# The first tile's gate, output rows and norm set apart from the second tile's in a two-layer decoder trunk

## Chip, cores and metric

One NeuronCore of a Trainium2 chip (trn2) runs the whole program. The metric is the device time of one execution in microseconds (us), here the median of three.

## What is computed

Two layers over 512 tokens of width 1024, float32, causal. Each layer is a token mixer with a residual and an expert FFN (PEER) with a residual, each behind an RMSNorm. Layer 0 mixes with HGRN2 (four heads of 128) and an S5 state-space model (32 groups, 64 states) whose output is gated; layer 1 with a gated DeltaNet. Cut to the parts around the change:

```python
# layer 0: the S5 half ends in a gate, then one output projection over both halves
y = gelu(y)
y = y * sigmoid(y @ glu_w)                      # "u" half of the mixer's output
h = h + concat(hgrn_out, y) @ ev_out_w          # output rows
# PEER FFN of both layers
xn = rmsnorm(h, norm_ffn_w)
q = (xn @ w_q).reshape(n_tok, 8, 2, 128)        # 8 heads, two halves
scores = einsum('thcd,ckd->thck', q, sub_keys)
top_s, top_i = top_k(scores, 16)                # then top 16 of the 256 sums
act = gelu(einsum('td,tkd->tk', xn, u_tab[expert_id]))
h = h + einsum('tk,tkd->td', gate * act, v_tab[expert_id])
```

## The kernel before, in words

Tokens lie along the free axis, channels on the 128 partitions. The mixer works on two groups of 256 tokens (g = 0, 1), the FFN on four tiles of 128 tokens. One round is one head of one tile: 16 slots, and in each slot GpSimd gathers 128 rows of 8 KB (the u and v rows of one expert for each token) into a ring of 8 (later 15) slots in SBUF (`gather`, L674 to 688), VectorE forms the dot products with the tile's rows (`dot`, L2318), ScalarE makes gelu and gate of two slots (`gelus`, L1523) and TensorE adds the weighted v rows in PSUM (`values`, L796), which releases the ring slots (`v_free`). There are 64 rounds, 1024 gathers. The ring's first eight slots (`ring`, L467) lie over the memory of the layer-0 mixer: slots 0 and 1 over chunks 0 to 3 of the output weights `first_w` (L384), slot 2 over `glu_w2[0]`, slots 3 to 5 over the S5 buffers, slots 6 and 7 over chunks 4 to 7 of `first_w`. So GpSimd waits before its first gather for `first_mm` = 4, which says that the output rows of both tiles of group 0 are done.

The order of work on each engine is written out by hand. `Paced` objects (L297) hold the steps of one piece of work with due slots, counted in slots of the round loop; negative slots, run through in a loop up to 0, are the stage ahead of the first gather. At each half slot the parts are called in the order of their list. `spread` (L140) maps the raw slots of the second group's mixer to slots, `query_at` (L87) sets where a query projection stands, `side_order` (L269) lists who uses the PSUM bank `side` and when. SyncE loads the weights through a ring of four (L594), each when the fourth before it has been used.

Ahead of the first gather, group 0 goes through the mixer. The norm of group 1 is made meanwhile (`second_norm`: squares on ScalarE from slot -112, L1440; eight matmuls with the mean matrix on TensorE at -104, L709; root on ScalarE, L1448), and applied on VectorE behind the gate (`mixer_in(1)`, L1944). `first_glu` (PE L1102, ACT L1655) makes the product with `glu_w` and the sigmoid for the whole group, `glu(0)` (L2197) the gate. Then TensorE runs `first_rows` (L1029) for tile 0 and tile 1 of the group interleaved: 4 k-blocks of a tile and one chunk of outputs are 4 matmuls; a float32 matmul shows as two records. VectorE adds the residual (`first_added`, L2215), ScalarE squares, TensorE sums (`first_sum`, L1046), ScalarE makes the root, VectorE applies it (`first_apply`, L1944), TensorE makes head 0's query (`first_query`, L1058) and scores (L1066). VectorE then routes (`route(0)`, L2239 to 2310), TensorE spreads the ids over the tile's blocks (`across`, L791), VectorE writes them (L2315), and the first gather goes. Behind it TensorE broadcasts the tile's rows (`first_tile_rows`, 32-row matmuls of 512 columns, L770; ScalarE copies them, L1508), sums tile 1's squares, and runs the queries of heads 0 and 1 for tile 1 (`two_heads`, L1080). These lines set the order on TensorE between the loops:

```python
first_rows(1, low, range(3))
pe.wait_ge(s["mixu_ready"], 2)
first_rows(0, high, range(DC))
first_rows(1, low, range(3, 6))
first_sum(0)
first_rows(1, low, range(6, DC))
first_rows(1, high, range(2))
first_query(0)
```

## Time and profile before

| | us |
|---|---|
| median of 3 runs | 3036.7 |
| lowest, highest | 3035.95, 3038.07 |
| span of the profiled execution | 3036.9 |
| TensorE, VectorE, ScalarE, GpSimd busy | 2117.2, 2207.9, 1402.1, 1164.2 |
| gathers: share of the 16 DMA engines' span | 85.8% |

The span runs from the first to the last instruction of the profiled execution; the page gives no other time of it, and it lies between the lowest and the highest of the three runs. No engine is busy for more than 73% of the span, while the DMA engines are busy most of it; the page's slices say where. Times in the rows below are in us from the span's start. PE is TensorE, PEld its weight loads, DVE VectorE, ACT ScalarE, POOL GpSimd, SP SyncE; PEclk is TensorE's granted clock as a share of 2.4 GHz.

### The profile page before, as it was taken

The page shows a single profiled execution, that of the slowest core. Times are in us where ns is not written, and L with a number is a line of the kernel's source. Part 1 is how long each engine was busy: PE and PEld are TensorE (multiplying, and loading weights), DVE is VectorE, ACT ScalarE, POOL GpSimd, SP SyncE. Part 2 cuts the span into 40 slices and gives each one's busy share as a digit, 9 for nine tenths or more (in the row PEclk, how much of TensorE's full clock was granted, in tenths as well). Part 3 has the DMA queues.
Part 4 walks back from the last instruction along what each step waited for, and adds up shares of the span by engine and source line. Part 5 has one row for each costly group of instructions (what it writes and reads, how often), then busy time and mean ns, then how long its engine had stood idle before and what let it go on. Part 6 is the DMA issues. An engine that isn't in the chain of part 4 may idle for free.

```text
span 3036.9 us, 39024 instructions
## 1 busy us (share of the span) xinstructions
PE 2117.2 (70%) x13544; PEld 1275.4 (42%) x13544; DVE 2207.9 (73%) x6050; ACT 1402.1 (46%) x3425; POOL 1164.2 (38%) x1041
## 2 busy tenths in 40 slices
PE   7989877674667688687776888868775655453334
PEld 6876544350334456455543655545442311120001
DVE  8767888767666878777666678878866766667774
ACT  3434455433234766674333476667433422342222
POOL 0013344444344434434334344344445344443342
PEclk8989887885789899988887889999886866575555
DMA  6239999999999999999999999999999999999997
GB/s 221 70 135 417 419 419 420 412 419 419 418 417 394 420 397 412 420 366 405 418 419 419 398 401 418 420 405 390 421 417 420 420 421 421 421 421 422 421 421 299
DMA packets 182422, 1185.28 MB, mean 390 GB/s; under 512 B 19664, under 2 KB 25808, under 8 KB 50896
## 3 DMA queue, kind: packets, MB, share of 16 engines
q0 software_dynamic: 147456, 1073.81, 85.8%
q1 hardware_dynamic: 34768, 108.98, 9.3%
q8 instruction: 107, 1.75, 0.2%
q14 instruction: 91, 0.75, 0.1%
HBM read 1180.61 MB, written 2.10 MB: 389 GB/s over the span
## 4 chain that ended last, share of the span: by engine, by line
DMA 43%; PE 28%; DVE 10%; ACT 9%; issue 5%; POOL 5%; another core or an unknown queue 0%; SPq 0%; DVEq 0%; ACTq 0%; POOLq 0%
DMA arena<-uv_tab,cols 42%; PE ps L805 7%; PE xps L728 6%; POOL arena L685 5%; DVE arena L2327 4%; PE ps L728 4%; ACT L1532 2%; ACT scr L1532 2%; PE xps L1214 2%; ACT scr L1536 1%; PE xps L1265 1%; PE ps L780 1%; DVE arena L2424 1%; PE xps L1288 1%; PE xps L1285 1%
## 5 line engine op out<-in xcount | busy, mean ns | idle before, releaser
L685 POOL DMA_INDIRECT arena<-uv_tab,cols x1024 | 1160.0, 1133 | 1828.0 <-PE ps L805 1265.0
L2327 DVE CUSTOM_DVE_ANT_0 arena<-arena 128x1024 f32<-128x1024 f32 x1024 | 1251.5, 1223 | 660.8 <-DMA arena<-uv_tab,cols 633.2
L805 PE MATMUL ps<-arena,scr 128*32 128x512 f32 x4096 | 717.6, 782 | 679.0 <-ACT scr L1536 649.1
L1532 ACT ACTIVATE scr<-sel,cols 128x32 f32<-128x32 f32 x1024 | 272.9, 314 | 1111.0 <-DVE cols L2327 1081.3
L805 PEld LDWEIGHTS ps<-arena,scr 128*32 128x32 f32 x4096 | 92.2, 121 | 1002.0 <-ACT scr L1536 897.2
L728 PE MATMUL xps<-arena,wring 128*128 128x256 f32 x1600 | 401.2, 401 | 8.7 <-DVE arena L2485 4.2
L728 PEld LDWEIGHTS xps<-arena,wring 128*128 128x128 f32 x1600 | 308.8, 200 | 102.9 <-issue 46.4
L728 PE MATMUL ps<-arena,wring 128*128 128x256 f32 x1152 | 293.6, 414 | 14.2 <-ACT arena L1497 7.6
L1536 ACT ACTIVATE scr<-scr,cols 128x32 f32<-128x32 f32 x1024 | 273.0, 313 | 16.6
L728 PEld LDWEIGHTS ps<-arena,wring 128*128 128x128 f32 x1152 | 235.1, 209 | 97.6 <-issue 41.9
L1532 ACT ACT_TABLE_LOAD x154 | 197.6, 1283 | 2.7
L780 PE MATMUL ps<-ident,arena 128*32 128x128 f32 x1792 | 75.7, 322 | 31.7 <-ACT arena L1515 25.9
L780 PEld LDWEIGHTS ps<-ident,arena 128*32 128x32 f32 x1792 | 60.9, 132 | 85.0 <-ACT arena L1515 56.3
L1265 PE MATMUL xps<-arena 128*128 128x128 f32 x448 | 69.1, 301 | 25.7 <-DVE arena L2437 23.1
L1265 PEld LDWEIGHTS xps<-arena 128*128 128x128 f32 x448 | 59.4, 205 | 62.0 <-DVE arena L2437 39.0
L2327 DVE DVE_READ_ACCUMULATOR2_ANT cols<- 128x1 f32 x1024 | 84.2, 82 | 0.0
L1521 ACT ACT_TABLE_LOAD x61 | 78.3, 1283 | 1.1
L2244 DVE FIND_INDEX8 cols<-cols,arena 128x8 uint32<-128x128 f32 x256 | 69.8, 285 | 0.0
L1515 ACT ACTIVATE arena<-ps 128x512 f32<-128x512 f32 x56 | 33.2, 594 | 78.1 <-PE ps L780 47.9
L2424 DVE SCALAR_TENSOR_TENSOR arena<-arena,consts 128x256 f32<-128x256 f32 x144 | 63.2, 480 | 7.2 <-ACT arena L1748 6.6
L1214 PE MATMUL xps<-arena 128*128 128x256 f32 x256 | 63.0, 397 | 6.7 <-DMA arena<-wall 6.7
L2239 DVE MAX8 cols<-arena 128x8 f32<-128x128 f32 x256 | 61.7, 283 | 7.5 <-ACT arena L1689 5.8
(462 smaller groups left out, 2713.3 us busy)
## 6 DMA issues: line engine op xcount, KB each, us to landing
wring<-wall SPq DMA_DIRECT2D x176, 512.0 KB
arena<-uv_tab,cols POOLq DMA_INDIRECT x1024
arena<-wall SPq DMA_DIRECT2D x16, 512.0 KB, 7.9
h<-xT SPq DMA_DIRECT2D x2, 1024.0 KB, 10.6
arena<-glu_w SPq DMA_DIRECT2D x2, 1024.0 KB
out<-arena SPq DMA_DIRECT2D x3, 512.0 KB
arena<-s_b SPq DMA_DIRECT2D x1, 512.0 KB, 9.0
arena<-s_bt SPq DMA_DIRECT2D x1, 512.0 KB, 9.7
```

Source lines behind the costliest of these rows:

```text
L685: pool.indirect_dma_start(out=whole_row(at), out_offset=None, in_=uv_tab, in_offset=bass.IndirectOffsetOnAxis(ap=ids[g % 2][:, k:k + 1], a ...
L728: mm = pe.matmul(o, wring[:, n % NSLOT, k, :], rhs[k], start=(first and k == 0), stop=(k == DC - 1), skip_group_check=True)
L780: mm = pe.matmul(side[32 * e:32 * e + 32, tl(k)], xn[:, 4 * (i % 2) + k, at:at + 32], ident[:, :], start=True, stop=True, skip_group_check ...
L805: mm = pe.matmul(ps[4 + half][32 * c:32 * c + 32, :], wdiag[:, b % PAIRS, j, :], pair_row(at + j, 1)[:, T * half:T * half + T], start=(g % ...
L1214: mm = pe.matmul(o, z_w[c][:, k, :], hm[:, k, :], start=(k == 0), stop=(k == DC - 1), skip_group_check=True)
L1265: mm = pe.matmul(ps[2][:, tl(j)], negA[:, tl(j)], inv[:, tl(j)], start=(j == 0), stop=(j == 3), skip_group_check=True)
L1521: act.activation(soft_e, sel_v, ACT.Exp, bias=soft_m, accum_out=soft_s).then_inc(s["soft_exp"], 1)
L1532: m = act.activation(wdiag[:, b % PAIRS, n % 2, :], place, ACT.Gelu, scale=dots[g % 2][:, n:n + 1])
L1536: m = act.activation(wdiag[:, b % PAIRS, n % 2, :], wdiag[:, b % PAIRS, n % 2, :], ACT.Copy, scale=gate[g % 2][:, n:n + 1])
L2244: m = dve.max_index(top_i[:, c, lo:lo + 8], top_v[:, c, lo:lo + 8], keyed[:, c, :])
L2327: dve.tensor_tensor_reduce(u, u, xrep[:, block_of(k), :], 1.0, 0.0, ALU.mult, ALU.add, dots[g % 2][:, k:k + 1]).then_inc(s["dot_done"], 1)
L2424: mm = stt(o, raw_in(i)[:, e, j:j + GT], conv_w[:, GH * i + 2 * p + e, j:j + 1], o, ALU.mult, ALU.add)
```

## The change

- Group 1's norm: its squares on ScalarE move from slot -112 to -83, into another buffer (`halves1`), its eight matmuls on TensorE from -104 to both sides of `first_sum(0)`, its root behind that of the first tile, its application on VectorE from behind the gate to behind the scaling of tile 0.
- `first_glu` is made by tile and not by output block; the sigmoids and the gate of tile 0 come first, each of half the size.
- The rows of tile 1 are no longer made ahead of tile 0's: 16 of their 64 matmuls stand behind tile 0's first query, 48 among the eight `first_tile_rows`. The residual add, the norm and the two heads' queries of tile 1 move to slots 3 to 9 of round 0.
- Tile 0's norm is applied in two steps, the product with the weight ahead of the root.
- Gathers use the ring turned by two slots, so that the first two take slots 2 and 3; gather 0 waits for `first_mm` = 2, gather 4 for 3, gather 6 for 4.
- Group 1's mixer starts at slot 11 and not 8 with a spread of 1.04 and not 1.05, head 2's query of group 0 at 12 and not 8, and `route(2)` runs in slots 18 to 21, three steps a slot, and no longer from slot 14.

The diff, cut to its core:

```diff
@@ -89,7 +89,7 @@
-    return 16 * r + (8 if r == 0 else 9 if r % 8 == 0 and r > 0 else 2)
+    return 16 * r + (12 if r == 0 else 9 if r % 8 == 0 and r > 0 else 2)
@@ -149,7 +149,7 @@
-SPREAD = {"even": (1, 8, 1.05, math.inf, 0), 0: (264, 264, 1.02, 380, 8), 1: (524, 524, 1.03, 637, 8)}
+SPREAD = {"even": (1, 11, 1.04, math.inf, 0), 0: (264, 264, 1.02, 380, 8), 1: (524, 524, 1.03, 637, 8)}
@@ -194,7 +194,7 @@
 def slot_of(at):
-    return at % NS if at < LONG_FROM else (at - LONG_FROM) % NS_LONG
+    return (at + 2) % NS if at < LONG_FROM else (at - LONG_FROM + 2) % NS_LONG
@@ -268,7 +268,7 @@
 def side_order():
-    todo = [(-10, "q", 0, -1), (-9, "sc", 0, -1), (-8, "q", 0, -2), (-7, "sc", 0, -2), (4.5, "q", 0, 0), (6.7, "sc", 0, 0)]
+    todo = [(-10, "q", 0, -1), (-9, "sc", 0, -1), (-8, "q", 0, -2), (-7, "sc", 0, -2), (8.5, "q", 0, 0), (10.7, "sc", 0, 0)]
@@ -380,7 +380,7 @@
-        halves1 = region(0, DC, GT)
+        halves1 = region(26112, DC, GT)
@@ -677,7 +677,9 @@
-            pool.wait_ge(s["first_mm"], 4)
+            pool.wait_ge(s["first_mm"], 2)
+    if g == 0 and k in (4, 6):
+        pool.wait_ge(s["first_mm"], 1 + k // 2)
@@ -701,23 +703,18 @@
         def _(pe):
-def norm_sum(g):
-    for k in range(DC):
+def norm_sum(g, ks):
+    for k in ks:
...
-        mm = pe.matmul(ps[(2, 6)[g]][:, 0:GT], mean_d[:, :], (halves, halves1)[g][:, k, :], start=(k == 0),
+        mm = pe.matmul(ps[(2, 0)[g]][:, 0:GT], mean_d[:, :], (halves, halves1)[g][:, k, :], start=(k == 0),
...
-    mm.then_inc(s["sum_ready"], 1)
+    if k == DC - 1:
+        mm.then_inc(s["sum_ready"], 1)
...
-norm_sum(0)
-def second_norm():
-    pe.wait_ge(s["u_ready"], 4)
-    norm_sum(1)
-    yield 0
+norm_sum(0, range(DC))
@@ -756,7 +753,8 @@
 def first_tokens():
-    pe.wait_ge(s["xn_first"], 1)
+    pe.wait_ge(s["xn_first"], 2)
+    pe.wait_ge(s["root_ready"], 2)
@@ -797,6 +795,8 @@
+    if g == 0 and b == 0:
+        pe.wait_ge(s["out_added"], 4)
@@ -1040,21 +1040,23 @@
 def first_sum(t):
-    for k in range(DC):
-        if k % 4 == 0:
-            pe.wait_ge(s["hsq_ready"], 2 * t + k // 4 + 1)
-        mm = pe.matmul(ps[(3, 5)[t]][:, 0:P], mean_d[:, :], first_sq2[t][:, k, :], start=(k == 0),
-                       stop=(k == DC - 1))
+    for n in range(DC):
+        k = n if t == 0 else (n + 4) % DC
+        if n % 4 == 0:
+            pe.wait_ge(s["hsq_ready"], 2 * t + n // 4 + 1)
+        mm = pe.matmul(ps[3][:, 0:P], mean_d[:, :], first_sq2[t][:, k, :], start=(n == 0),
+                       stop=(n == DC - 1))
...
 def first_query(hd):
...
-    pe.wait_ge(s["xn_first"], 1)
...
+            if k % 4 == 0 and c == 0:
+                pe.wait_ge(s["xn_first"], k // 4 + 1)
@@ -1066,6 +1068,11 @@
+def tile_one_sum():
+    first_sum(1)
+    yield 0
@@ -1101,32 +1108,27 @@
 def first_glu():
-    def part(ks, n):
-        o = ps[(0, 5)[n // 2]][:, GT * (n % 2):GT * (n % 2) + GT]
+    def part(ks, t):
...
-            mm = pe.matmul(o, glu_w2[0][:, k, P * n:P * n + P], uT[:, k, :], start=(n % 2 + k == 0),
-                           stop=(k == 3), skip_group_check=True)
+            for n in range(4):
+                mm = pe.matmul(ps[(0, 5)[t]][:, tl(n)], glu_w2[0][:, k, P * n:P * n + P], uT[:, k, tl(t)],
+                               start=(n + k == 0), stop=(k == 3), skip_group_check=True)
...
-    pe.wait_ge(s["root_ready"], 2)
-    for n in (0, 1):
-        part(range(3), n)
+    part(range(3), 0)
...
-    for n in (2, 3):
-        part(range(3), n)
+    part(range(3), 1)
...
-    for n in range(4):
-        mm = part((3,), n)
-        if n % 2:
-            mm.then_inc(s["s5_glu"], 1)
+    for t in range(2):
+        part((3,), t).then_inc(s["s5_glu"], 1)
@@ -1348,7 +1350,7 @@
-        pe.wait_ge(s["mixu_ready"], 3)
+        pe.wait_ge(s["mixu_ready"], 5)
@@ -1366,11 +1368,11 @@
-paced += [Paced(-147.5, pair_weights()), Paced(-104, second_norm())]
+paced += [Paced(-147.5, pair_weights())]
...
-paced += [Paced(-80, first_glu()), Paced(mixed_at(1) + 1, glu(1), g_slot(1)), Paced(3.25, two_heads())]
+paced += [Paced(-80, first_glu()), Paced(mixed_at(1) + 1, glu(1), g_slot(1)), Paced(4.5, tile_one_sum()), Paced(7.25, two_heads())]
@@ -1381,24 +1383,29 @@
-pe.wait_ge(s["s5_xy"], ST)
-first_rows(1, low, range(3))
...
-first_rows(1, low, range(3, 6))
+pe.wait_ge(s["s5_sig"], 2)
+norm_sum(1, low)
...
-first_rows(1, low, range(6, DC))
-first_rows(1, high, range(2))
+norm_sum(1, high)
...
-first_rows(1, high, range(2, DC))
+pe.wait_ge(s["s5_xy"], ST)
+first_rows(1, low, high)
...
+pe.wait_ge(s["mixu_ready"], 4)
...
-first_sum(1)
+    if i < 4:
+        first_rows(1, high, (4 + i,))
+    elif i < 6:
+        first_rows(1, low, range(2 * i - 8, 2 * i - 6))
+    else:
+        first_rows(1, high, range(2 * i - 12, 2 * i - 10))
@@ -1444,16 +1451,14 @@
-    root = (trt, nrt)[g]
-    own.link(act.activation(root, ps[(2, 6)[g]][:, 0:GT], ACT.Ln, bias=eps_col))
-    act.activation(root, root, ACT.Exp, scale=-0.5).then_inc(s["root_ready"], 1)
-def second_norm():
-    act.wait_ge(s["mixh_ready"], 1)
+    own.link(act.activation(trt, ps[(2, 0)[g]][:, 0:GT], ACT.Ln, bias=eps_col))
+    act.activation(trt, trt, ACT.Exp, scale=-0.5).then_inc(s["root_ready"], 1)
+def second_squares():
+    act.wait_ge(s["e_mm"], 20)
...
-    yield 12
-    norm_root(1)
+    yield 0
@@ -1659,22 +1664,24 @@
-    for i in range(2):
-        yield 14 + i
-        act.wait_ge(s["s5_glu"], i + 1)
-        act.activation(sg[:, 2 * i:2 * i + 2, :], heads2(ps[(0, 5)[i]][:, :]),
-                       ACT.Sigmoid).then_inc(s["s5_sig"], 1)
+    for t in range(2):
+        for i in range(2):
+            yield 14 + 2 * t + i
+            act.wait_ge(s["s5_glu"], t + 1)
+            act.activation(sg[:, 2 * i:2 * i + 2, tl(t)], tiles4(ps[(0, 5)[t]][:, :])[:, 2 * i:2 * i + 2, :],
+                           ACT.Sigmoid).then_inc(s["s5_sig"], 1)
 def first_norm(t):
-    for i in range(2):
-        act.wait_ge(s["out_added"], 2 * t + i + 1)
+    for n in range(2):
+        i = (n, 1 - n)[t]
+        act.wait_ge(s["out_added"], 2 * t + n + 1)
...
+    yield 1.5
...
-    act.wait_ge(s["hm_ready"], 4)
-    own.link(act.activation(nrt[:, tl(t)], ps[(3, 5)[t]][:, 0:P], ACT.Ln, bias=eps_col))
+    own.link(act.activation(nrt[:, tl(t)], ps[3][:, 0:P], ACT.Ln, bias=eps_col))
@@ -1859,10 +1866,10 @@
-paced += [Paced(-147, pair_weights()), Paced(-112, second_norm())]
+paced += [Paced(-147, pair_weights()), Paced(-83, second_squares())]
...
-paced += [Paced(-81.5, first_glu()), Paced(mixed_at(1), glu(1), g_slot(1)), Paced(5.25, two_heads())]
+paced += [Paced(-81.5, first_glu()), Paced(mixed_at(1), glu(1), g_slot(1)), Paced(4, first_norm(1)), Paced(9.25, two_heads())]
@@ -1871,7 +1878,9 @@
-first_norm(0)
+for _ in first_norm(0):
+    pass
+norm_root(1)
@@ -1881,7 +1890,6 @@
-first_norm(1)
@@ -1991,7 +1999,7 @@
-        norm_apply(0, (trt, nrt)[g], h[:, :, own_tokens(g)], hm,
+        norm_apply(0, trt, h[:, :, own_tokens(g)], hm,
@@ -2197,29 +2205,51 @@
 def glu(g):
+    if g:
+        dve.wait_ge(s["s5_sig"], 6)
+        for i in range(2):
+            x = uT[:, 2 * i:2 * i + 2, :]
+            mm = tt(x, x, sg[:, 2 * i:2 * i + 2, :], ALU.mult)
+        mm.then_inc(s["mixu_ready"], 1)
+    else:
+        first_gate(0)
+def first_gate(t):
...
-        dve.wait_ge(s["s5_sig"], 2 * g + (2 if g else i + 1))
-        x = uT[:, 2 * i:2 * i + 2, :]
-        mm = tt(x, x, sg[:, 2 * i:2 * i + 2, :], ALU.mult)
-        if i or g == 0:
-            mm.then_inc(s["mixu_ready"], 1)
-    if g == 0:
-        mixer_in(1)
+        dve.wait_ge(s["s5_sig"], 2 * t + i + 1)
+        x = uT[:, 2 * i:2 * i + 2, tl(t)]
+        tt(x, x, sg[:, 2 * i:2 * i + 2, tl(t)], ALU.mult).then_inc(s["mixu_ready"], 1)
 def first_added(t):
...
-    for i in range(2):
-        dve.wait_ge(s["first_mm"], 2 * t + i + 1)
+    for n in range(2):
+        i = (n, 1 - n)[t]
+        dve.wait_ge(s["first_mm"], 2 * t + n + 1)
...
+def first_weighted(i):
+    dve.wait_ge(s["out_added"], i + 1)
+    mark(tt(xn[:, 4 * i:4 * i + 4, tl(0)], h[:, 4 * i:4 * i + 4, tl(0)],
+            norm_w[:, 1, 4 * i:4 * i + 4].unsqueeze(2).to_broadcast([P, 4, P]), ALU.mult))
+def first_scaled():
+    settled()
+    dve.wait_ge(s["h_root"], 1)
+    for i in range(2):
+        x = xn[:, 4 * i:4 * i + 4, tl(0)]
+        tt(x, x, nrt[:, tl(0)].unsqueeze(1).to_broadcast([P, 4, P]), ALU.mult).then_inc(s["xn_first"], 1)
 def first_apply(t):
...
-               range(DC)).then_inc(s[("xn_first", "xn_ready")[t]], 1)
+               range(DC)).then_inc(s["xn_ready"], 1)
@@ -2535,12 +2565,15 @@
+first_gate(1)
...
-first_apply(0)
+for i in range(2):
+    first_weighted(i)
+first_scaled()
+mixer_in(1)
...
-first_added(1)
@@ -2548,17 +2581,23 @@
-        if r == 0 and k == 1:
+        if r == 0 and k == 3:
+            first_added(1)
+        if r == 0 and k == 5:
...
-        if k == (14 if r % PH == 0 else ROUTE_SLOT):
+        if r and k == (14 if r % PH == 0 else ROUTE_SLOT):
...
+        if r == 1 and k == 2:
+            nxt = route(2)
...
-        if k % 2 == 0:
+        if k % 2 == 0 or r == 1 and k < 5:
+            next(nxt, None)
+        if r == 1 and k < 5:
```

## Rows read from the trace of the kernel before

**Rows 1.** The page, section 2: slices of 75.9 us (1/40 of the span).
```profile
PEclk8989887885789899988887889999886866575555
DMA  6239999999999999999999999999999999999997
GB/s 221 70 135 417 419 419 420 412 419 419 418 417 394 420 397 412 420 366 405 418 419 419 398 401 418 420 405 390 421 417 420 420 421 421 421 421 422 421 421 299
```
**Rows 2.** The page, section 3: queue, packets, MB, share.
```profile
q0 software_dynamic: 147456, 1073.81, 85.8%
```
**Rows 3.** Windows: length, busy us of each engine (instructions), PEclk, DMA share, GB/s.
```profile
118.00:124.00 6.00, 5.72 (x62) 4.16 (x61) 1.88 (x6) 4.43 (x6) 0.00 (x0) 1.00 0.28 90
...
200.00:203.00 3.00, 3.00 (x10) 1.23 (x9) 2.90 (x14) 1.56 (x3) 2.38 (x3) 0.97 0.46 93
203.00:210.00 7.00, 7.00 (x11) 2.60 (x10) 4.71 (x16) 3.00 (x6) 5.47 (x6) 0.50 0.98 404
...
200.00:220.00 20.00, 15.59 (x44) 7.48 (x43) 10.95 (x39) 11.43 (x20) 8.68 (x8) 0.66 0.92 367
220.00:235.00 15.00, 14.51 (x109) 11.91 (x106) 12.86 (x36) 7.16 (x22) 6.08 (x6) 0.89 1.00 385
250.00:600.00 350.00, 273.43 (x1782) 170.81 (x1775) 290.37 (x865) 176.10 (x407) 144.29 (x124) 0.85 1.01 418
```
**Rows 4.** Timeline, GpSimd: start us, us, line, what, idle before and its releaser.
```profile
200.01 1.09 POOL L685 DMA_INDIRECT arena<-uv_tab,cols  x1 [195.43 <-DVE cols L2315]
...
220.63 0.93 POOL L685 DMA_INDIRECT arena<-uv_tab,cols  x1 [9.81 <-PE ps L805]
...
285.25 0.94 POOL L685 DMA_INDIRECT arena<-uv_tab,cols  x1 [10.53 <-PE ps L805]
```
**Rows 5.** Chain that ended last, 0 to 260 us: start us, us, what.
```profile
112.19 3.65 PE ps L709 x16
...
165.94 2.68 PE xps L1036 x24
168.62 3.57 PE ps L1036 x32
172.19 4.47 PE xps L1036 x40
...
180.23 1.79 PE ps L1036 x16
...
183.81 3.59 PE ps L1058 x32
...
200.47 10.46 PE xps L770 x16
```
**Rows 6.** Timeline: ScalarE, VectorE and TensorE, 100 to 166 us.
```profile
101.87 2.00 ACT L1440 ACTIVATE arena<-h 128x1024 f32<-128x1024 f32 x2
...
148.25 0.38 ACT L1647 ACTIVATE arena<-ps 128x256 f32<-128x256 f32 x1 [10.07 <-PE ps L1022]
...
150.71 0.42 ACT L1653 ACTIVATE arena<-arena 128x256 f32<-128x256 f32 x1
...
151.34 0.48 DVE L2193 SCALAR_TENSOR_TENSOR arena<-ps,consts,arena 128x256 f32<-128x256 f32 x1
...
161.31 0.50 PE L945 MATMUL xps<-arena 128*128 128x128 f32 x2 [0.74 <-DVE arena L2140]
...
163.91 1.28 ACT L1665 ACT_TABLE_LOAD   x1
```
**Rows 7.** Groups by form, 163 to 200 us: shapes, count, busy us, mean ns, idle.
```profile
L1944 DVE SCALAR_TENSOR_TENSOR arena<-h,consts,rt 128x256 f32<-128x256 f32 x8 | 3.3, 480 | 0.0
...
L2215 DVE TENSOR_TENSOR h<-h,xps 128x512 f32<-128x512 f32 x2 | 1.4, 682 | 2.9 <-PE xps L1036 2.9
...
L1672 ACT ACTIVATE arena<-h 128x512 f32<-128x512 f32 x2 | 1.3, 630 | 9.3 <-DVE h L2215 9.3
```
**Rows 8.** Timeline, ScalarE: a copy of a broadcast row at full clock.
```profile
202.42 0.60 ACT L1508 ACTIVATE arena<-xps 128x512 f32<-128x512 f32 x1 [0.26 <-PE xps L770]
```

## The prediction, made before the change was run

> **What bounds the kernel now.** I read the slices of the page first. From slice 4 on the DMA engines are busy in nine tenths or more of nearly every slice and move 417 to 422 GB/s in most of them; only the first three slices and the last lie far below [rows 1]. The traffic is the 1024 gathers of the expert rows, 1073.81 MB in all [rows 2], so 1.05 MB each and 2.5 us each at 420 GB/s. Between 250 and 600 us the mean is 418 GB/s at a share of 1.01 [rows 3]. So from the first gather on the end is set by bytes, and a change of this kind is worth what it moves the stream of gathers, plus or minus any gap it opens or closes in that stream.
>
> Then the timeline around the first gather: it is issued at 200.01, after 195.43 us in which GpSimd only waited for the routing (the reader is to see the bracket) [rows 4]. In 200 to 220 the engines move 367 GB/s x 20 us, in 220 to 235 another 385 x 15 [rows 3]: 7.3 MB and 5.8 MB. At 420 GB/s the first is what a stream beginning at 202.5 would have moved (so a gather takes 2.5 us from issue to flow), and both together what one beginning at 203.8 would have: another 1.3 us is lost in 220 to 235, where gather 8 is issued only at 220.63 and the queue behind it is thin [rows 4].
>
> Last, the chain up to there. Up to the last heads of the mixer it is TensorE, with the eight matmuls of the second group's norm on it at 112.19 [rows 5]; then VectorE's last S5 states, up to the read-out that waits for them at 161.31 [rows 6]; then gelu, sigmoid, the gate, the first tile's output rows, its norm, the first query, and the routing [rows 5, 6].
>
> **The change, part by part.** All times are of the profiled execution, whose span is 3036.9, 0.2 above the median of 3036.7.
>
> Second group's norm, early half. Its eight matmuls (16 records) leave the chain at 112.19: 3.65 us [rows 5]. TensorE waits for no one there, ScalarE's next steps follow it, and its weights were asked for three weights earlier, so I take all of it: -3.65. ScalarE's two squares and its table load and root leave too, beside that chain, at no gain.
>
> Squares put later. The two squares, 2.00 us as a pair at 101.87 [rows 6], now come due at slot -83, where ScalarE also has the root of head 3; of two parts due together the one listed first goes first, so the squares go ahead of that root. Its Square ends at 148.63, the root at 151.13, and the VectorE instruction that wants it starts at 151.34 [rows 6]. Behind that one in VectorE's order stand the last three states, which set the end of this stretch. So 2.0 less 0.2 of slack, less up to 0.2 that the Ln waited for TensorE's sum in any case: +1.6 (ends 1.4 and 1.8). The Gelu of three blocks is 1.7 late as well, but TensorE reaches its read-out of the last states (161.31) within the same shift [rows 6].
>
> Gate of the first tile alone. From the sigmoid's table load at 163.91 to the first of the 32 matmuls (64 records) of the first tile's u half at 168.62 are 4.71 us [rows 5, 6]. On that path now stand 1.28 of load, two sigmoids of 128x256 at 0.38 (as the Square of that size from PSUM) and a last gate of 0.48 at most (the nearest 128x256 product) [rows 6], with hand-offs 2.6. The 12 matmuls of the second tile (2.68 at 165.94 [rows 5]) that stood in front are gone. -2.1.
>
> Norm of the first tile. These 32 matmuls end at 175.76 and the first query begins at 183.81, 8.05 later, with 28 matmuls of the second tile and the 8 of the sum between. Now there are four norm matmuls of 256 columns (half of 3.65, 1.83), the sum (16 records, 1.79) and the other four (1.83): 5.45 [rows 5]. The other way round, add and square take 1.4 and hide behind the first 1.83; root, and weighted product (0.68 of 128x512, made ahead) and scaling need 1.5 after the sum, under the second 1.83. -2.6. The second group's eight apply steps (3.3 [rows 7]) now stand ahead of the routing on VectorE, but the query, its copy and the scores take over 5 us: hidden, with about 1 us to spare; without that cover up to 1 us comes back. The query's path from 183.81 to the gather stays as it is, 16.2 us; TensorE, with 16 matmuls of the second tile and the second query beside the routing, is ready for the ids some 1.5 us early.
>
> Sum: -3.65 + 1.6 - 2.1 - 2.6 = -6.8. The first gather at 193.2.
>
> The wait that is added. The turned ring lets gathers 0 to 3 go at once; 4 and 5 need the chunks 4 to 7 of the second tile's rows, 6 and 7 all of them, and everything behind on GpSimd's queue waits too. Six gathers flow from 195.7 to 210.7. TensorE begins its interleaved stage 0.4 after the first gather: eight broadcasts of the first tile's rows at 0.86 (idle 0.26 and copy 0.60 of one step [rows 8]) and 48 matmuls (96 records, 10.7 at 1.79 for 16): 17.6, to 211.2. Chunks 4 to 7 are done by 200.6, in time. Gather 6 is issued at 211.2 and flows at 213.7: a gap of 3.0. That wait isn't bounded by before's trace, which never had a gather held in mid-ring; its ends are 0.5 (no start-up) and 3.0 plus what the clock may cost, below. Next: the products of gathers 0 and 1 wait for the add of the second tile (211.9), so gathers 8 and 9 go at 213.5 and 214.8, with four in the queue; the two heads' queries, now at slot 7.25, start near 221.7 and hold back gathers 14 and 15 to some 232, when the queue lasts to 238 with the four weight loads that the queries release. So the 1.3 us of thin queue in 220 to 235 should go: -1.3 (end: 0).
>
> Second group's mixer 3 slots later and route(2) packed into slots 18 to 21: before, GpSimd waits 10.53 us at 285.25 just behind this stretch [rows 4], with the DMA still full; packing adds some 1.6 us there, but takes half a projection of 3.8 us from in front of the products. Nothing, with ends -0 and +2.
>
> Total: -6.8 + 3.0 - 1.3 = -5.1: 3031.8 for that execution, **3031.6 for the median**, 0.17% less.
>
> **The clock in the interleaved stage.** In 203 to 210, TensorE is busy for 7.00 of 7.00 us with broadcasts alone and its granted clock is 0.50, the level of 1.2 GHz; in 118 to 124, where 32-row matmuls stand among 128-row ones, it is 1.00, 2.4 GHz [rows 3]. The new stage is a mix like the second, so I cost it at 2.4 GHz. The Trainium skill ("TensorE: Matmul & The Clock Gate", the HAM clock gate) says that activity releases the throttle and idleness brings it on; by that rule alone the stage would stay at full clock, and the sum would be the one above. The row of 203 to 210 speaks against it: busy is not enough there.
>
> **Rivals.** (1) *The stage runs at 1.2 GHz throughout* (slower): place, the 17.6 us between ids and fourth semaphore; for it, the clock of the broadcasts [rows 3] and 1.5 us of idle TensorE before it; against, the 128-row half. Price: 17.6 more, gather 6 at 228.8: -5.1 + 17.6 = +12.5, 3049.2. It turns the sign beyond 5.1 us of excess and is slower by over 0.2% beyond 11.2. (2) *The gain is cut, not lost*: 7 us of the stage at half clock, as from 203 to 210, gives +3.5 (3035.1); the packed routing opening a gap, or VectorE's cover gone, 1 to 3. That is also the case in which the rows of the second tile do not follow the gathers but hold them. (3) *Gather 6 starts faster than the first one did.* In 200 to 203 the engines moved 93 GB/s [rows 3], but the engines were empty; issued beside running ones, its start-up may be hidden: the gap is 0.5, the change -7.6, 3029.1. The skill's page "DMA: Bandwidth & Descriptors" (Anatomy of one DMA) puts most of a software DMA's fixed cost at its completion, not its start, with a first byte after about 1 us; that rule would give nearly this case. The trace does not agree: it puts the start at 2.5 for the only gather where it can be seen [rows 3, 4]. (4) *Errors of the chain in the good direction*: the squares cost less, or the 2.4 GHz level holds through the stretch near 141: 1 to 2 more, about 3030.
>
> **Numbers.** Forecast, 3030.7 to 3033.5: 0.37. Cases 3 and 4, 3027.5 to 3030.6: 0.18 and 0.14. Case 2, 3033.5 to 3042: 0.23. Case 1, above 3042.8: 0.08. A measurement of this kernel can tell about 0.2% (6.1 us), so faster is below 3030.6: 0.32; slower 0.08; same 0.60. The range, 3027.5 to 3038.5, leaves out the far part of case 2 and case 1, and a little below.
>
> **What would show it.** First gather near 193; the L2193 of head 3 idling 1.5 us for its root; first query near 177; a wait of GpSimd ended by L1036 before gather 6 near 211 and a dent in the GB/s there of some 3 us; no dent at 222; TensorE's clock at 1.00 from 193 to 211. If the first gather is at 193 and the end has not moved by some 5 us, the gap is what I mis-sized; if the first gather is late, the chain is.

## The result, and the profile after

The change makes the kernel slower: 3048.4 us against 3037.9 us, medians of five runs each on one chip, ratio 1.0034 with a 95% interval of 1.0023 to 1.0044. The repeat on another chip, below, agrees. The profiled execution has a span of 3043.2 us (time 3045.0, the lowest of the five, so some 3 us below the median); its end is 6.3 later than that of the profiled execution of the kernel before.

The page after, the same lines as [rows 1, 2]:

```profile
PEclk8989887785688899898887999989886866565555
DMA  6229999999999999999999999999999999999997
GB/s 220 70 106 404 417 413 420 419 419 421 414 417 409 413 397 405 415 372 399 419 419 419 412 394 419 419 419 384 421 420 420 420 421 421 421 420 422 421 421 298
...
q0 software_dynamic: 147456, 1073.81, 85.6%
```

The bytes are the same, and 28 of the 35 slices from the fifth to the 39th stand at 412 to 422 GB/s, with a few lower ones among them in both kernels. What is new lies in the third and the fourth slice: 106 and 404 GB/s where [rows 1] has 135 and 417. So the loss is at the head of the stream, as the argument on bytes said it would be. GpSimd's timeline there (start us, us, line, what, idle before and its releaser), to be held against [rows 4]:

```profile
190.62 1.09 POOL L687 DMA_INDIRECT arena<-uv_tab,cols  x1 [186.03 <-DVE cols L2345]
...
206.49 1.96 POOL L687 DMA_INDIRECT arena<-uv_tab,cols  x1 [10.98 <-PE ps L1036]
...
221.26 0.94 POOL L687 DMA_INDIRECT arena<-uv_tab,cols  x1 [10.81 <-PE xps L1036]
...
224.12 1.80 POOL L687 DMA_INDIRECT arena<-uv_tab,cols  x1 [0.30 <-issue]
...
232.70 1.08 POOL L687 DMA_INDIRECT arena<-uv_tab,cols  x1 [5.54 <-PE ps L805]
```

These are gathers 0, 4, 6, 8 and 10. The first is 9.4 us earlier than before. But four gathers are 10 us of traffic, and gather 4 comes 15.9 us after gather 0; the next two are another 5 us, and gather 6 comes 14.8 after gather 4. By gather 8 the lead is gone (224.12 against 220.63). Windows of the same stretch (length, busy us of PE, PEld, DVE, ACT, POOL with instructions, PEclk, DMA share, GB/s) show the two holes, and why they are so long:

```profile
191.00:203.00 12.00, 12.00 (x31) 6.84 (x30) 5.47 (x24) 1.94 (x4) 3.60 (x4) 0.51 0.88 343
203.00:212.00 9.00, 9.00 (x29) 5.95 (x28) 5.34 (x12) 1.19 (x2) 3.66 (x2) 0.52 0.33 104
...
206.00:208.00 2.00, 2.00 (x4) 0.50 (x2) 1.99 (x7) 0.00 (x0) 1.51 (x1) 0.50 0.00 0
212.00:221.00 9.00, 8.99 (x54) 6.28 (x54) 0.00 (x0) 3.12 (x5) 0.00 (x0) 1.00 0.36 140
...
218.00:222.00 4.00, 2.99 (x18) 2.04 (x18) 0.97 (x4) 2.89 (x6) 0.74 (x1) 1.00 0.00 0
...
225.00:245.00 20.00, 14.54 (x96) 10.04 (x96) 11.70 (x33) 7.55 (x19) 7.83 (x6) 0.74 0.94 350
250.00:600.00 350.00, 284.27 (x1768) 178.50 (x1768) 287.58 (x857) 172.03 (x401) 138.90 (x122) 0.82 1.01 417
```

TensorE is busy without a break from 191 to 212, and its granted clock is 0.51: the interleaved stage runs at 1.2 GHz for its first 21 us. The DMA engines move nothing from 206 to 208 and from 218 to 222: gathers 4 and 6 wait for the second tile's rows, which this slow stage makes. TensorE's own timeline shows the chain up to the stage, and the stage at both clocks:

```profile
161.67 3.84 PE L1036 MATMUL ps<-arena 128*128 128x128 f32 x32 [0.44 <-DVE arena L2222]
...
174.28 3.81 PE L1060 MATMUL ps<-arena,wring 128*128 128x128 f32 x32
...
189.82 0.27 PE L789 MATMUL ps<-scr,sel 128*32 128x32 f32 x8 [1.61 <-DVE scr L2340]
...
190.66 1.53 PE L768 MATMUL xps<-arena 32*128 32x512 f32 x2
192.12 2.08 PE L1036 MATMUL ps<-arena 128*128 128x128 f32 x8
194.13 2.07 PE L768 MATMUL xps<-arena 32*128 32x512 f32 x2
...
214.85 1.12 PE L768 MATMUL xps<-arena 32*128 32x512 f32 x2
215.91 2.05 PE L1036 MATMUL xps<-arena 128*128 128x128 f32 x16
```

At 194.13 a broadcast (two records, 32*128) takes 2.07 us and at 214.85 it takes 1.12; eight records of the second tile's rows take 2.08 at 192.12, sixteen take 2.05 at 215.91. The stage lasts from 190.66 to 221.0, 30.3 us, where the sum had 17.6.

**One number for the stream.** Because the rest of the run is bound by bytes, the bytes moved up to 340 us say when an unbroken stream of 420 GB/s would have had to begin: 340 - 160 x G / 420, with G the mean GB/s from 180 to 340 us. Two windows, first of the kernel before, then of the changed one:

```profile
180.00:340.00 160.00, 141.83 (x843) 99.25 (x841) 113.74 (x356) 64.73 (x155) 53.51 (x49) 0.89 0.88 357
```
```profile
180.00:340.00 160.00, 142.77 (x792) 97.61 (x790) 102.80 (x320) 64.42 (x148) 53.20 (x47) 0.87 0.84 336
```

That gives 204.0 and 212.0 (each to 0.2 us). The change delays the stream by 8.0 us, 0.26% of the time; the measured ratio has 0.23 to 0.44%. The first gather is worth -9.4; gaps between 200 and 225 cost 15.4, gaps from 225 to 245 another 3.3, and those after that 0.3, where the kernel before lost 1.6 in all: -9.4 + 19.0 - 1.6 = +8.0. Behind 340 us nothing is lost: from the begin of the stream to the end of the span are 2832.9 us before (3036.9 - 204.0) and 2831.2 in the changed kernel.

### The profile page after: what moved, and what is told of

Same layout as the page of the kernel before. It is cut to its first block, busy times and chain, and to the rows that moved or that the text cites. A ratio compares the mean times of both kernels' runs of the same rounds, so it can differ in the third digit from the quotient of the medians.

```text
span 3043.2 us, 39092 instructions
## 1 busy us (share of the span) xinstructions
PE 2133.7 (70%) x13576; PEld 1282.2 (42%) x13576; DVE 2209.1 (73%) x6048; ACT 1404.9 (46%) x3430; POOL 1168.0 (38%) x1041
## 4 chain that ended last, share of the span: by engine, by line
DMA 44%; PE 28%; DVE 12%; ACT 8%; POOL 5%; issue 4%; SPq 0%; DVEq 0%; ACTq 0%; POOLq 0%
DMA arena<-uv_tab,cols 43%; PE xps L725 7%; PE ps L805 7%; DVE arena L2357 5%; POOL arena L687 5%; PE ps L725 4%; PE xps L1216 2%; ACT scr L1537 2%; ACT L1537 1%; ACT scr L1541 1%; PE xps L1267 1%; PE xps L1290 1%; PE xps L1287 1%; DVE arena L2454 1%; DMA arena<-wall 1%
## 5 line engine op out<-in xcount | busy, mean ns | idle before, releaser
L2467 DVE COPY_PREDICATED arena<-arena,xps 128x512 f32<-128x512 uint32 x72 | 48.5, 720 | 18.5 <-PE xps L1290 14.1
```

## The experiments

All ratios are to the kernel before, run on the same chip in between. The runs of one kernel spread over 6 to 12 us, so the intervals are 0.1% to each side. The figure for the stream from the window of 180 to 340 us is finer and stands beside each; it comes from one profiled execution of each kernel.

**The stage: order, gap, form.** Three kernels each change one thing about the stage, and a fourth run repeats the changed kernel.

First, the order alone:

```diff
+            first_rows(1, high, high)
+            first_rows(1, low, low)
+            first_rows(1, high, low)
             for i in range(8):
                 first_tile_rows(i)
-                if i < 4:
-                    first_rows(1, high, (4 + i,))
...
```

> All 48 matmuls of the second tile's rows stand ahead of the eight broadcasts, nothing else is altered. Theory A (the broadcasts among the matmuls hold the clock down, and gathers 4 to 7 wait for the last of them): the 48 matmuls run at 2.4 GHz or after one spell at 1.2 GHz, 11 to 14 us, gather 6 is issued by 205, the gap at 203 to 209 and that at 215 to 223 go, the broadcasts end near 212 and gather 8 follows at 213: 3028 to 3034. Theory B (packed routing): 3044 to 3048, little changed.

Measured: ratio 1.0000 (0.9991 to 1.0009), gather 6 at 202.59, stream as if begun at 205.1. TensorE's timeline and a window of this run:

```profile
195.01 7.31 PE L1036 MATMUL xps<-arena 128*128 128x128 f32 x64
202.25 10.09 PE L768 MATMUL xps<-arena 32*128 32x512 f32 x16
```
```profile
191.00:203.00 12.00, 12.00 (x102) 11.61 (x103) 3.60 (x20) 0.38 (x1) 6.26 (x7) 1.00 0.81 312
...
204.00:206.00 2.00, 2.00 (x6) 0.72 (x6) 1.10 (x1) 1.20 (x3) 0.77 (x1) 0.99 1.04 438
206.00:208.00 2.00, 2.00 (x4) 0.96 (x4) 1.97 (x7) 0.68 (x2) 0.00 (x0) 0.50 0.98 414
```

The 96 records of 128 rows run at 1.00 in spite of the same 1.6 us of idle ahead of them. The eight broadcasts behind them start at 1.00 and fall to 0.50 with no idle time before the fall. So it is not idleness alone: the broadcasts bring the clock down by themselves. The time was missed by theory A as by B: the median is 3041.2 where the kernel before takes 3041.9 on that chip. Gather 6 came by 205, as A said, but gather 8 at 217.70 and not 213.

Second, the gap filled: two chunks of the second tile's rows go between the second query and the ids, so that TensorE isn't idle there.

```diff
             first_query(1)
+            pe.wait_ge(s["mixu_ready"], 4)
+            first_rows(1, high, (4, 5))
             across(0)
...
+                if i < 2:
+                    continue
                 if i < 4:
                     first_rows(1, high, (4 + i,))
```

> Two of the chunks (8 matmuls) are moved from the stage to the idle 1.6 us of TensorE ahead of the spreading of the ids. Theory A1 (the idle gap brings the clock down): it stays at 2.4 GHz through the stage, which takes 18 us, gather 6 near 209, 3032 to 3036. Theory A2 (the 32-row broadcasts bring it down and hold it): 1.00 up to the first broadcasts, then 0.50 again, the stage a mere 4 us shorter (two chunks at half clock), 3040 to 3046.

```profile
191.16 1.95 PE L1036 MATMUL ps<-arena 128*128 128x128 f32 x16
193.04 0.27 PE L789 MATMUL ps<-scr,sel 128*32 128x32 f32 x8
...
193.88 2.93 PE L768 MATMUL xps<-arena 32*128 32x512 f32 x6
196.74 1.16 PE L1036 MATMUL ps<-arena 128*128 128x128 f32 x8
197.83 1.12 PE L768 MATMUL xps<-arena 32*128 32x512 f32 x2
```
```profile
191.00:203.00 12.00, 12.00 (x73) 7.94 (x72) 7.45 (x34) 3.75 (x7) 6.14 (x6) 1.00 0.60 220
203.00:212.00 9.00, 9.00 (x55) 6.46 (x54) 5.54 (x12) 2.95 (x4) 0.00 (x0) 1.00 0.96 401
```

The broadcasts are still of 32 rows, there is no idle time before them, and the clock stays at 1.00 to the end of the stage at 212.1, as theory A1 said. The edit does two things at once: it takes the idle time away and it puts 16 records of 128 rows there, so that three broadcasts follow each other without rows between them. Which of the two keeps the clock up is not shown. Ratio 0.9992 (0.9983 to 1.0001), stream at 204.8; the first gather was late in this execution (193.84), so gather 6 came at 212.44 and not near 209.

Third, the form: the same product with a stationary operand of 128 rows that holds zeros outside the block of 32, written by VectorE ahead of the first tile's add. It computes the same rows.

```diff
-                r = slice(32 * (i // 2), 32 * (i // 2) + 32)
-                pe.matmul(ps[i % 2][:, :], place4[r, :, :].rearrange("p e j -> p (e j)"), ycur[r, T * (i % 2):T * (i % 2) + T],
+                if i == 0:
+                    pe.wait_ge(s["whole_ready"], 4)
+                pe.matmul(ps[i % 2][:, :], whole[:, i // 2, :], ycur[:, T * (i % 2):T * (i % 2) + T],
...
+            mark(dve.memset(whole, 0.0))
+            settled()
+            for b in range(4):
+                r = slice(32 * b, 32 * b + 32)
+                dve.tensor_copy(whole[r, b, :].rearrange("p (e j) -> p e j", e=4), place4[r, :, :]).then_inc(s["whole_ready"], 1)
```

> The eight broadcasts of the first tile's rows take all 128 rows of the array: the stationary operand is 128x128 with zeros outside the block's 32 rows, made on VectorE in five small instructions while it waits for the first rows (1.5 us at most). Same columns, same order. Theory A2 (a 32-row matmul counts for little in the clock's favour): the clock is 1.00 in the stage but for at most one spell after the idle gap; the stage takes 18 to 22 us, 3031 to 3038. Theory A1 (the idle gap alone): 0.50 over the stage as in the changed kernel, 3045 to 3053.

```profile
190.65 0.27 PE L791 MATMUL ps<-scr,sel 128*32 128x32 f32 x8 [1.61 <-DVE scr L2342]
...
191.40 1.02 PE L770 MATMUL xps<-arena 128*128 128x512 f32 x2
192.25 1.05 PE L1038 MATMUL ps<-arena 128*128 128x128 f32 x8
```
```profile
191.00:203.00 12.00, 12.00 (x74) 9.13 (x75) 7.34 (x30) 3.97 (x7) 5.85 (x6) 1.00 0.79 292
```

The idle 1.61 us are there, the clock is 1.00, and the stage lasts from 191.40 to 209.15: 17.75 us, as the prediction's sum had it (17.6). Gather 6 is issued at 209.42. Ratio 0.9983 (0.9974 to 0.9992), stream at 202.1, 9.9 us earlier than in the changed kernel. The clock is as theory A2 said, and A1 (the idle time alone) is out. The change that was made, with its stage at 2.4 GHz, does not lose: this is the experiment that names the cause.

The repeat of the changed kernel:

> The changed kernel once more, unaltered, for a second profile. Its five times lay between 3044.97 and 3053.31 us, and the profiled execution was the fastest of them. Theory A (the low clock of the interleaved stage costs the time): a slower execution than 3045 has a longer stretch of 1.2 GHz in the stage or behind it, so the fourth first_mm comes at 221 or later and gather 112 lies 10 us or more behind the one of the kernel before. Theory B (the packed routing or the later mixer costs it): the stage and gather 6 are as before, and the gathers fall back after gather 16.

Ratio 1.0030 (1.0018 to 1.0042), gathers 0, 4 and 6 at 192.12, 208.00 and 222.77, again a stage of 30 us, stream at 213.5, and gather 112 at 529.98 where the kernel before has it at 518.59: theory A. The stream stands 21.4 us behind its first gather, exactly as in the first profile (212.0 and 190.62).

**A control in the kernel before.** The same 128-row broadcasts put into it, nothing else:

> The kernel before with the 128-row broadcasts and nothing else. If the 32-row form alone brings the clock down, its 8 broadcasts at 203 to 210 now run at 1.00 and take 8 x 0.5 = 4 us instead of 7 or more, and nothing else changes up to the first gather (200.0). The time: at most the 1.3 us of thin queue can be won, so within 0.1% of the kernel before; ratio 0.9993 to 1.000. If instead this form is cheaper for the whole kernel (the theory that the 0.17% under before of the broadcasts-only kernel is not from the change at all), the ratio here would be about 0.998 too.

```profile
200.48 7.32 PE L772 MATMUL xps<-arena 128*128 128x512 f32 x16
```

The eight broadcasts take 7.3 us where [rows 5] has 10.46 for the same sixteen records of 32 rows, and the clock is 1.00 from 200 to 210. The 4 us that were expected were missed, because the broadcasts and ScalarE's copies (0.60 us each [rows 8]) wait for each other in turn. They were not of use to the time: ratio 1.0004 (0.9995 to 1.0013), stream at 203.6 against 204.0. So the form of the broadcasts is a cure for the stage of the changed kernel and not a gain of its own.

**What the turned ring is worth.** The 128-row kernel with the ring as it was, the first gather waiting for all four groups of the second tile's rows:

```diff
-    return (at + 2) % NS if at < LONG_FROM else (at - LONG_FROM + 2) % NS_LONG
+    return at % NS if at < LONG_FROM else (at - LONG_FROM) % NS_LONG
...
-                        pool.wait_ge(s["first_mm"], 2)
-                if g == 0 and k in (4, 6):
-                    pool.wait_ge(s["first_mm"], 1 + k // 2)
+                        pool.wait_ge(s["first_mm"], 4)
```

> The 128-row broadcasts with the ring not turned: slots from 0 and gather 0 waiting for the fourth of the first matmul groups. Everything else as in the changed kernel. Both theories of the stage: ids near 191, but the first gather only when the 17.6 us of the stage are over, near 209.5, and no gap after it; the stream as if begun at 212 to 213 at 260 us, some 11 us later than with the ring turned, so a time of 3047 to 3049 and a ratio of 1.002 on the chip where the kernel before takes 3041.9: the turned ring is worth about 11 us once the stage stands behind the first gather. If instead the six early gathers only take bytes forward that the later gap gives back, the two differ by less than 4 us.

```profile
211.59 1.09 POOL L686 DMA_INDIRECT arena<-uv_tab,cols  x1 [207.00 <-PE xps L1036]
```
```profile
229.36 1.94 PE L805 MATMUL ps<-arena,scr 128*32 128x512 f32 x8 [18.70 <-DVE h L2231]
```

Ratio 1.0051 (1.0037 to 1.0064), the slowest of all, stream at 217.7 where 212 to 213 was expected. The first gather came 2 us later than expected, and the loss after it was missed: TensorE now idles 18.7 us for VectorE's add of the second tile, which stands in VectorE's order behind the dot products of the first gathers, and the products after that take 1.94 us for eight records, the rate of 1.2 GHz, where the changed kernel has 1.07 at 222.11. With the stage behind the ids, the turned ring is worth 15.6 us of stream.

**The thin queue behind the stage.** The 128-row kernel still gives back 4.1 us between 215 and 245. Six kernels change the order there. The second tile's rows ahead of the broadcasts, its sum and norm among them and the two heads' queries as before the change:

```diff
             for i in range(8):
+                if i == 4:
+                    first_sum(1)
                 first_tile_rows(i)
...
-                    if r == 0 and k == 5:
+                    if r == 0 and k == 1:
                         first_apply(1)
...
```

> The changed kernel with the 128-row broadcasts, and the second tile put back to where it holds less: its 48 matmuls go ahead of the broadcasts, its sum and its norm between broadcasts 3 and 4, its products on VectorE at slot 1 of round 0, and the two heads' queries at slots 3.25 and 5.25 as before the change. My theory now (two errors: TensorE's clock in the stage, and a thin queue behind it, because the sum at 4.5 stands in front of the weight values of slots 0 and 1 and the queries are late): first gather near 191.5, granted clock 1.00 through the stage, gather 6 issued near 203 instead of 209.4, gather 10 near 216 instead of 220.5, no stretch under 300 GB/s between 215 and 245; the stream at 260 us as if begun at 197 to 199 (201.7 with the broadcasts alone changed), so the time 3 to 5 us below that kernel, 3032 to 3034 where the kernel before takes 3041.9, ratio 0.9968 to 0.9978. The rival (what stands between the first gather's 9 us and the end is lost elsewhere: the transfers are paced by something else than their issue) says: no more than 1 us below it, ratio 0.998.

Missed: ratio 0.9996 (0.9987 to 1.0005), stream at 202.9 where 197 to 199 was expected. Of the miss 2.1 us are there at the first gather (193.51 for 191.44 in the 128-row kernel); behind it the edit brings 1.3. Gather 6 came early, at 204.61, but gather 8 only at 219.51: the broadcasts now end at 214.7, because the second tile's squares and root stand between them on ScalarE, and the first products wait for ScalarE behind them.

Only the sum moved, from slot 4.5 to slot 5:

> The 128-row broadcasts, and of the second tile only its sum moved, from slot 4.5 to slot 5, behind the weight values of slots 0 and 1. Thin-queue theory: those values no longer wait for the sum and ScalarE's squares, gather 10 is issued near 216 to 217 instead of 220.5, and the stream at 260 us is as if begun at 199.5 to 200.5 instead of 201.7; time 1 to 2 us less than with the broadcasts alone, ratio to the kernel before 0.9975 to 0.998. Rival (the queries at 7.25, not the sum, make the queue thin): gather 10 moves, gathers 14 to 16 do not, and the stream at 260 stays at 201.5 to 202, ratio 0.9983.

Missed too: ratio 1.0000 (0.9991 to 1.0009), stream at 206.7 where 199.5 to 200.5 was expected. Of the 4.6 us over the 128-row kernel 3.5 are there at the first gather (194.92 for 191.44), ahead of the edit; the edit itself costs 1.1. Gathers 8 to 10 came closer together (215.75 and 220.32, where the 128-row kernel has 212.27 and 220.51), and the whole wait went to gather 12 (231.62 for 226.80), because VectorE now stood 7.7 us in the scaling of the second tile and not 6.4.

So two theories for this stretch were set against each other: VectorE, which waits in that scaling (V), or ScalarE with its table loads (S). Sum, scaling and queries later, with the 128-row broadcasts:

```diff
-... Paced(4.5, tile_one_sum()), Paced(7.25, two_heads())]
+... Paced(5, tile_one_sum()), Paced(8.25, two_heads())]
...
-                    if r == 0 and k == 5:
+                    if r == 0 and k == 7:
                         first_apply(1)
```

> The 128-row broadcasts; the second tile's sum at slot 5, its scaling on VectorE at slot 7 instead of 5, the two heads' queries at 8.25 and 10.25 instead of 7.25 and 9.25. Theory V (what makes the queue thin is VectorE: in the kernel with the broadcasts alone changed it waits 6.4 us, from 213.3 to 219.67, in the scaling at slot 5 for ScalarE's root, and the products of gathers 5 to 7 stand behind it): the products go on, the stream at 240 us is as if begun near 199 instead of 201, and the time is about 2 us less than with the broadcasts alone, ratio to the kernel before near 0.9975. Theory S (ScalarE binds: its five table loads of 1.28 us for gelu, the routing's exponential and the norm's root stand between the weight values whatever the order): gathers 10 to 16 move by less than 2 us and the stream at 240 stays at 200.5 to 201.5, ratio 0.998 to 0.9985.

That edit and, ahead of it, the 48 matmuls of the second tile in front of the broadcasts (the diff of the rows-first kernel):

> As the kernel with the scaling at slot 7, and the 48 matmuls of the second tile ahead of the broadcasts. Gather 6 at 203 to 204.5 (before it, no gap: six gathers flow until 209), first products at 206 to 207, gather 8 near 214 to 215, while the eight issued flow until about 216: the gap of 2.6 us at gather 6 goes. Theory V: as if begun near 197 to 198 at 240 us, ratio 0.9965 to 0.997, the best of all. Theory S: the products come 5 us later than in the mixed order and the queue empties at 215 to 220 instead: 201 to 202.5, as with the second tile's norm put early, ratio 0.9985 to 0.9995.

The later sum, scaling and queries alone, in the changed kernel with its 32-row broadcasts:

> The changed kernel as it is, 32-row broadcasts included, with the scaling at slot 7, the sum at 5 and the two heads' queries at 8.25 and 10.25. The stage stays at 1.2 GHz in both theories (gather 6 near 221 to 222, 30 us after the first gather). Theory V: of the 3.4 us that the stream loses from 225 to 245 some 2 come back, time 3046 to 3047 where the changed kernel has 3048 to 3049, ratio 1.0022 to 1.0028. Theory S: nothing, 1.0034.

The 128-row broadcasts and rows first, with sum, scaling and queries where the change has them:

> The changed kernel with the 128-row broadcasts and the 48 matmuls of the second tile ahead of them, nothing else. The two cures of the stage's clock should not add up: the clock is 1.00 with either. Gather 6 at 202 to 203.5 and no gap there (2.6 us less than with the broadcasts alone), the products start near 206; the sum at 4.5 and the scaling at 5 are as before, so the thin queue stays or grows. Stream as if begun at 200 to 202 at 240 us, ratio 0.998 to 0.999. If the order alone is what keeps the rows-first kernel with 32-row broadcasts at 1.000, whatever the clock, the ratio would be 1.000 again.

Measured, ratio and stream: scaling later 0.9998 (0.9989 to 1.0007), 202.1; scaling later and rows first 0.9993 (0.9984 to 1.0002), 201.3; scaling later with the 32-row broadcasts 1.0029 (1.0017 to 1.0041), 213.5; rows first alone 0.9994 (0.9985 to 1.0003), 205.5. Held against what was expected, neither theory comes out whole. The pair with rows first differs by the later sum, scaling and queries alone, and they bring 4.2 us of stream, 0.6 of it there already at the first gather (193.16 for 193.73). So VectorE's place counts in that order; but V had expected 197 to 198, and 201.3 lies in the range of S. In the mixed order VectorE's wait in the scaling falls from 6.4 us to 0.9, and that brings 1 to 2 us: from 200 to 250 us that kernel loses 5.2, the one without the edit 6.3, and behind their first gathers the two lose 9.0 and 10.7. Both theories had expected a ratio of 0.9985 or less. With the stage at 1.2 GHz 1.1 us come back from 225 to 245 (363 GB/s for 340 in the repeated changed kernel) and are lost again by 340 (213.5 in both, with first gathers at 192.17 and 192.12). Rows first alone was expected at 200 to 202 and came at 205.5. With the scaling out of the way TensorE's products show whom they wait for, first in the mixed order:

```profile
216.23 1.94 PE L807 MATMUL ps<-arena,scr 128*32 128x512 f32 x8 [3.06 <-ACT scr L1543]
...
224.80 1.94 PE L807 MATMUL ps<-arena,scr 128*32 128x512 f32 x8 [3.01 <-ACT scr L1543]
```

Of ScalarE's timeline in the kernel with both edits (columns: start us, us), the loads stand one behind the other; five in 13 us:

```profile
211.80 1.28 ACT L1536 ACT_TABLE_LOAD   x1
...
214.21 1.28 ACT L1525 ACT_TABLE_LOAD   x1
...
215.93 1.28 ACT L1536 ACT_TABLE_LOAD   x1
...
219.38 1.28 ACT L1681 ACT_TABLE_LOAD   x1
...
223.60 1.28 ACT L1536 ACT_TABLE_LOAD   x1
```

No run took these loads away, so that they bind is read from the waits and not tried, and what holds this stretch stays open in part.

All kernels in one table, in the order of the stream. The third column is where the first gather was issued, the fourth what the stream lost behind it (it holds the first gather's own start of some 2.5 us), the fifth what the stream alone says, 1 + (begin - 204.0) / 3037:

| kernel | stream as if begun at | first gather | behind it | says | measured |
|---|---|---|---|---|---|
| rows first, 128 rows, scaling later | 201.3 | 193.16 | 8.1 | 0.9991 | 0.9993 |
| 128 rows | 202.1 | 191.44 | 10.7 | 0.9994 | 0.9983 |
| 128 rows, scaling later | 202.1 | 193.09 | 9.0 | 0.9994 | 0.9998 |
| 128 rows, second tile early | 202.9 | 193.51 | 9.4 | 0.9996 | 0.9996 |
| before, with 128 rows | 203.6 | 200.19 | 3.4 | 0.9999 | 1.0004 |
| before | 204.0 | 200.01 | 4.0 | 1 | 1 |
| gap filled | 204.8 | 193.84 | 11.0 | 1.0003 | 0.9992 |
| rows first | 205.1 | 191.49 | 13.6 | 1.0004 | 1.0000 |
| rows first, 128 rows | 205.5 | 193.73 | 11.8 | 1.0005 | 0.9994 |
| 128 rows, sum at 5 | 206.7 | 194.92 | 11.8 | 1.0009 | 1.0000 |
| changed kernel | 212.0 | 190.62 | 21.4 | 1.0026 | 1.0034 |
| changed kernel, repeated | 213.5 | 192.12 | 21.4 | 1.0031 | 1.0030 |
| 32 rows, scaling later | 213.5 | 192.17 | 21.3 | 1.0031 | 1.0029 |
| ring unturned | 217.7 | 211.59 | 6.1 | 1.0045 | 1.0051 |

Up to the first gather the changed kernels differ little (the gap filled and the ring unturned apart), and yet it comes between 190.62 and 194.92. That is the execution and not the edit: from ScalarE's Square of head 3 to the first gather are 48.59 us alike in the changed kernel, its repeat, the rows-first and the 128-row kernel. The fourth column is free of it. There the three profiles with the slow stage stand together at 21.3 and 21.4, and the 128-row broadcasts alone take 10.7 us off.

Every measured ratio lies within 0.0011 of what its stream says. Only the interval of the 128-row kernel lies below 1; those of the gap filled and of the two kernels with rows first and 128 rows reach up to 1.0001, 1.0002 and 1.0003. By its stream the best kernel gains 2 to 3 us, 0.06 to 0.09%. The 0.17% of the 128-row kernel is one session, and more than its stream explains, and the kernel with the scaling later, whose stream is the same, measured 0.9998: that it is real is not shown.

## Why the prediction was wrong

The forecast was 3031.6, 5.1 less than before, with a range of 3027.5 to 3038.5; it came out at 3048.4, 10.5 more than the kernel before in the same session. Step by step:

**The chain up to the first gather** was right part by part, and the sum of -6.8 came out at -9.4. The head-3 steps of ScalarE and VectorE after, for [rows 6]:

```profile
142.03 0.38 ACT L1652 ACTIVATE arena<-ps 128x256 f32<-128x256 f32 x1 [8.71 <-PE ps L1022]
142.31 1.99 ACT L1447 ACTIVATE arena<-h 128x1024 f32<-128x1024 f32 x2
...
146.12 0.42 ACT L1658 ACTIVATE arena<-arena 128x256 f32<-128x256 f32 x1
```
```profile
146.57 0.48 DVE L2201 SCALAR_TENSOR_TENSOR arena<-ps,consts,arena 128x256 f32<-128x256 f32 x1 [1.27 <-ACT arena L1658]
```

- Second norm off the chain: the Square of head 3 moved from 148.25 to 142.03, -6.2 for a forecast of -3.65. The matmuls are 3.45 of it: TensorE is 1.40 earlier ahead of their old place (107.79 for 109.19) and 4.85 behind it (112.55 for 117.40). The 1.40 are there already at 100 us; they need no edit, for the kernel before with 128-row broadcasts is 1.5 later than the kernel before at the same place (98.56 for 97.08), with the same work ahead of it. The last 1.4 is the spell of 1.2 GHz at 141, which this execution doesn't meet: ScalarE is idle 8.71 us ahead of that Square and not 10.07. Three of the later kernels meet two such spells, between 137 and 156, and issue their first gather at 193.8, 194.9 and 193.7; seven with the same edits and no spell there issue it between 191.4 and 193.5, on average 1.7 earlier. This was rival 4, and it came true here; but these 2.8 us of the -9.4 are luck of the execution. Over the eleven profiles with this front (all but the ring unturned) the first gather comes at 192.7 on average, near the 193.2 of the forecast.
- Squares later: from the Square to VectorE's use 4.54 us, before 3.09: +1.45 for +1.6. The squares do go ahead of the root.
- Gate of the first tile: its 32 matmuls start at 161.67, 6.95 earlier than before, and VectorE's use of the head-3 root was 4.77 earlier: -2.2 for -2.1.
- Norm of the first tile: the query starts at 174.32, 9.5 earlier: -2.5 for -2.6. From there to the gather 16.3 for 16.2.

**The stage behind the ids is the step that failed.** "The new stage is a mix like the second, so I cost it at 2.4 GHz", 17.6 us, and therefore a gap of 3.0. It took 30.3 us, and the gaps up to 225 us are 15.4. The size without the clock was right: with 128-row broadcasts it takes 17.75. What was wrong is the comparison: the stretch of 118 to 124 has other 32-row matmuls in other work, and the rows of 203 to 210 [rows 3] and the 1.5 us of idle time that the text itself named pointed the other way. The case was there as rival 1, with its price (17.6 us more, 3049.2 in all) within 1 us of the outcome, and was given a chance of 0.08. The price comes close by errors that cancel, and as a difference it is 2 us off (+12.5 for +10.5): the clock was low for 21 us of the stage and not throughout, at a cost of 12.7 us and not 17.6, gather 6 came at 221.26 and not at 228.8, and the thin queue, two items on, cost 3.3 where the price had a gain of 1.3.

Rule and row, once more: by the Trainium skill ("TensorE: Matmul & The Clock Gate", the HAM clock gate) activity releases the throttle. These runs do not agree: from 191 to 203 TensorE was busy 12.00 of 12.00 us, and the granted clock was 0.51.

**The gap without the clock** (3.0, with 0.5 as rival 3's) can be read in the 128-row kernel: six gathers flow from 193.9, until 209.0, gather 6 is issued at 209.42, and the stream loses 2.2 us between 205 and 215. From 209 on the engines move 238, 41 and 229 GB/s in three windows of 1 us: a gather that is issued when the queue has run empty pays for its start again. Rival 3 is out; 3.0 was near.

**The term -1.3 for the thin queue was wrong in sign.** It was taken that gathers 8 and 9 go as soon as the second tile is added, and that four in the queue carry over the rest. In the changed kernel gathers 8 and 9 do go at 224.12 and 226.22, and then the second tile's sum, its scaling and the two heads' queries stand in the way of the products: 3.3 us lost from 225 to 245, where the forecast had none and the kernel before lost 1.3 (220 to 235). With the stage at 2.4 GHz it is 4.1 us from 215 to 245. Here is what held it in the 128-row kernel, VectorE's waits (what, total us, times, longest) and TensorE's sum:

```profile
DVE arena L1954 <- ACT rt L1687: 6.4, 1, 6.4
```
```profile
215.10 3.79 PE L1049 MATMUL xps<-arena,mean_d 128*128 128x128 f32 x16 [3.58 <-ACT arena L1681]
```

The sum waits for ScalarE's squares, which stand behind the weight values of slots 0 to 3 and three table loads; it then runs at 1.2 GHz (3.79 us for sixteen records that take 1.79 at the other level [rows 5]); and VectorE waits 6.4 us in the scaling, with the products of the next slots behind it. The prediction followed the add and the semaphores of the gathers through this stretch, but not ScalarE's order, and in front of the products it had the two heads' queries and not the sum and the scaling.

**Packed routing and the mixer three slots later** at 0, with ends -0 and +2: from 245 to 340 us the stream of the changed kernel loses 0.3, so no gap opened there. The 128-row kernel loses 1.1 there, most of it from 250 to 265 (402, 398 and 386 GB/s in windows of 5 us); whether that is the packed routing was not tried. Behind 340 nothing shows: the 2832.9 us from the begin of the stream to the end are 2831.2 and 2833.7 in the two profiles of the changed kernel. No run took these two parts of the change away alone.

Put together with what was measured in the 128-row kernel, which is the change as the prediction thought of it: first gather -8.6, gap 2.2, thin queue 4.1, 1.9 at the very start and after 245, less the 1.6 that before lost in all: -2.0, as the streams have it (202.1 against 204.0), where the forecast had -5.1. So with the clock right the forecast would still have been 3 us too good.

## What to carry to other kernels

When work is moved behind an event that starts a transfer, cost it at TensorE's lower clock as well, unless the trace shows the very same mix of shapes, with the same idle time ahead of it, at the higher one; busy alone proves nothing. Here two remedies kept the clock up: the small matmul form padded with rows of zeros, and the gap in front of it filled with work that is due later anyway. And a stream of transfers started early is only worth what the engines behind it can keep up: follow each in-order engine (the one with table loads too) until the lead has been spent or kept, not just to the first transfer.
